# Hybrid decoder step: block-diagonal level scores, step widths in column strips, regrouped banks, vector loads on another queue

## The chip, the cores and the metric

One core of one Trainium2 chip runs the kernel. The metric is device microseconds of one execution. TensorE (PE) multiplies, VectorE (DVE), ScalarE (ACT) and GpSimd (POOL) work on elements, and SyncE (SP) issues DMAs. The engines run side by side and meet only at semaphores.

## The reference

Two decoder layers run over a prompt of 256 tokens and 8 sample sequences of 4 tokens, 288 tokens together. Everything is float32. Each layer has three token mixers on the same normalised input (HGRN2, Mamba-2 SSD, dilated attention), an output projection, and then a dense SwiGLU (layer 0) or top-2-of-8 experts (layer 1). The parts that the change touches:

```python
fgate = lb + (1.0 - lb) * sigmoid(hf)                  # HGRN2: S_t = diag(f_t) S_{t-1} + k_t v_t^T
rel = where(causal, G[:, :, None] - G[:, None, :], -inf)    # G = cumsum(log f)
attn = einsum('bthd,bshd,btshd->bhts', q, k, exp(rel))      # scores within a chunk
...
dt = softplus(dt_raw + dt_bias)                        # SSD step width, dt_raw = 8 columns of h @ w_in
y, s_ssm = ssd_recurrence(xs, dt, -exp(a_log), bm, cm, ssm_h0)
...
qg, kg = rms_norm(q, q_norm[g]), rms_norm(k, k_norm[g])     # attention, groups g = 0, 1, 2
```

## The kernel before

Features lie on partitions and tokens along the free dimension, so a product of one weight tile with all tokens is a matmul with a 128x128 stationary tile and 288 moving columns. A float32 matmul appears in the trace as two instructions, each with its own weight load.

**The mixer loop.** `mixer(L)` on TensorE runs over 70 projection tiles t (`proj_tile`, L960: eight matmuls, 16 instructions) and after each tile does the small products that belong to it (`small_products`, L1257). Two tiles share a weight slab of 1 MB, and four slabs circulate in a ring that SP fills. Constants at the top (L56 to L60) say after which t each small product comes. The other engines run their own loops in the same order, so the schedule is written by hand. Results go into eight PSUM banks: tiles rotate through banks 5 to 7 (`acc_job`), small products have fixed banks 0 to 4 (`plan_mixer`, L322). `open_bank` (L922) waits until the bank's previous content has been read (`drained`), and `close_bank` tells readers that it is filled.

**Level scores (t = 19 to 33).** The HGRN2 scores are exact without large exponents because they are built by levels of distance h = 1, 2, 4, ..., 128 (`LEVELS`). For level i DVE computes distances and multiplies the queries (`hgrn_levels`, L2291), ACT takes the exponential (`level_decay`, L1818), POOL multiplies the keys (L862), and TensorE multiplies keys with queries in `level` (L1021): two blocks of 128 tokens, four heads, each 128x128. DVE then copies the wanted entries from PSUM under a mask (`level_mask`, L2274, `copy_predicated`). The mask of level h has ones only inside diagonal blocks of 2h tokens, and the "same" product (distance 0, t = 20) only on the diagonal. Levels 0, 1 and "same" have a further part for the sample tokens. Level 7 (h = 128) is a product of one block with the other.

**Step widths (t = 27).** `contract(("dt", L), wdt, ...)` (L1481) multiplies the eight columns of the step widths with all 288 tokens in eight matmuls. ACT copies the result (L2038), and DVE starts on it in `dt_start` (L2380).

**Second means and token rows (t = 47 to 51).** `hgrn_means` at 47, then `qk_means` (L1249) of attention group 1 at 48. ACT makes its squares at t = 47 (`qk_squares`, L1907), right behind `hgrn_rstd`, and its inverse roots at t = 48 (`qk_rstd`). At 50 `ssd_x_rows` turns x into token rows, three blocks in banks 3, 4, 3. At 51 `ssd_b_rows` (L1151) turns B, three blocks in banks 0, 1, 2, and makes two products "cb" in banks 3 and 4. DVE reads all of these in `ssd_rows` (L2398), after `qk_normed(L, 1)`.

**Start.** SP issues three loads of x, then 28 small loads of vectors (L636 to L651), then the first four weight slabs (L608), `wdt` and the convolution state. TensorE turns x and then the vectors, ACT copies both out of PSUM, DVE multiplies x with the gain (L2219), and `proj_tile` 0 needs these gained tiles and the first slab. POOL builds constants meanwhile (L796 to L844).

Of the kernel before, what the change touches and what calls it, by code (L numbers as in the profile page):

```python
# [56 lines left out]
AT_HEAD, AT_QK, AT_HG_MEAN = (38, 40, 43, 45), (42, 48, 62), 47  # L57
AT_XTOK, AT_BTOK, AT_EVENT, AT_SSM_ST, AT_STATE, AT_SSM_MEAN, AT_KV = 50, 51, 52, 54, (55, 58, 61, 64), 67, 69
QK_BANKS = ((4, 0, 2, 1), (4, 0, 2, 1), (0, 1, 2, 3))
# [24 lines left out]
def hybrid_decoder(nc, x_prompt, x_sample, state_hgrn, state_ssm, state_conv, cache_kv_w128, cache_kv_w512,  # L84
# [6 lines left out]
    with ctx:  # L91
# [141 lines left out]
        halfm = sb("halfm", [P, DB // 2])  # L233
        own_row = sb("own_row", [P, 2, 4 * DS])
# [87 lines left out]
        def plan_mixer(L):  # L322
            job(("norm", L, 0), 0)
            for t in range(N_PROJ):
# [5 lines left out]
                if t == AT_DT:  # L330
                    acc_job(("dt", L))
                i = (t - AT_LEVEL) // 2
# [34 lines left out]
                if t == AT_XTOK:  # L367
                    for b in range(3):
                        job(("xtok", L, b), 3 + b % 2)
                if t == AT_BTOK:  # L370
                    for b in range(3):
                        job(("btok", L, b), b)
# [225 lines left out]
        def _(sp):  # L598
# [37 lines left out]
            for L in range(DEPTH):  # L636
                vr = arena[:, 3 * D + P * L:3 * D + P * L + P]
                rows = [(V_MIX, mix_norm[L].rearrange("(a p) -> a p", p=P)),
                        (V_FFN, ffn_norm[L].rearrange("(a p) -> a p", p=P)),
                        (V_CW, ssm_conv_w[L].rearrange("j (a p) -> (j a) p", p=P)),  # L640
                        (V_CB, ssm_conv_b[L].rearrange("(a p) -> a p", p=P)),
                        (V_SN, ssm_norm[L].rearrange("(a p) -> a p", p=P)),
                        (V_HN, hgrn_norm[L:L + 1, :]),
                        (V_LB, hgrn_lb_logits[L].rearrange("(a p) -> a p", p=P))]
                for r, src in rows:
                    sp.dma_start(vr[r:r + src.shape[0], :], src).then_inc(vecs_in, 16)  # L646
                for r, src in ((V_QN, att_q_norm[L]), (V_KN, att_k_norm[L])):
                    for e in range(2):
                        sp.dma_start(vr[r:r + AG, 64 * e:64 * e + 64], src).then_inc(vecs_in, 16)
                for k, src in enumerate((ssm_dt_bias, ssm_a_log, ssm_d)):  # L650
                    sp.dma_start(hv[:, L, k:k + 1], src[L].rearrange("(h a) -> h a", a=1)).then_inc(vecs_in, 16)  # L651

            for L in range(DEPTH):
# [129 lines left out]
        def _(pool):  # L783
# [22 lines left out]
            for i, h in enumerate(LEVELS[:7]):  # L806
# [14 lines left out]
                                  pattern=[[DS, DB]], channel_multiplier=-1))  # L821
# [2102 lines left out]
```

## Time and profile before

| | us |
|---|---|
| median of 3 runs (2321.06 to 2325.76) | 2322.9 |
| the profiled execution, as timed | 2326.01 |
| its span in the trace | 2324.3 |
| TensorE busy in the span | 2278.7 (98%) |
| mean granted TensorE clock | 0.992 of full speed |

The profiled execution's time is its span and 1.7 us around it. The rows further down are lines of this one execution. A timeline row gives start, duration, engine, line of the kernel, operation, what it writes and reads with shapes (partitions x elements), how many instructions it merges, and in brackets how long the engine had been idle before it and who ended that. L935 and L941 are the helpers through which all matmuls go, L1794 that of all activations, so what a row is has to be read from its shapes and its place.

### The profile page before, as it was taken

To read this page: it belongs to the slowest core of one execution; us is meant where nothing else is said; L and a number is where in the kernel's file an instruction comes from. 1 tells how busy PE (TensorE), PEld (TensorE's weight loads), DVE (VectorE), ACT (ScalarE), POOL (GpSimd) and SP (SyncE) were. 2 spreads that over 40 slices of the span, in tenths; PEclk is the share of its full clock that TensorE was granted. 3 is DMA by queue.
4 is the path that set the end of the run, shared out by engine and by line. 5 is a ranking of instruction groups with operands and counts; after the bars stand their busy time and mean duration, and the time that the engine had idled before them with its cause. 6 is when DMAs were issued, how large, how long until landed. Compare 5 with 4: busy or idle time off the path is not lost.

```text
span 2324.3 us, 43998 instructions
## 1 busy us (share of the span) xinstructions
PE 2278.7 (98%) x19656; PEld 1454.2 (63%) x19656; DVE 580.8 (25%) x1141; ACT 410.8 (18%) x777; POOL 132.3 (6%) x149
## 2 busy tenths in 40 slices
PE   8999999999999999999999989999999999999998
PEld 6777777767777778777776744354444534353535
DVE  4384324432110127633253210101010010101000
ACT  3323324301000132332331110000000000000000
POOL 2121120000000002111100000000000000000000
PEclk9999999989999999999999999999999999999999
DMA  4334536564444543343476099999999899989993
GB/s 153 125 105 132 151 121 171 140 181 127 131 135 112 153 138 109 118 145 105 136 202 188 19 383 412 418 381 341 384 375 377 339 364 396 361 344 360 396 364 119
DMA packets 290396, 535.20 MB, mean 230 GB/s; under 512 B 10936, under 2 KB 222010, under 8 KB 273824
## 3 DMA queue, kind: packets, MB, share of 16 engines
q1 hardware_dynamic: 290208, 532.38, 64.9%
q8 instruction: 156, 2.56, 0.4%
q14 instruction: 32, 0.26, 0.0%
HBM read 518.50 MB, written 13.85 MB: 229 GB/s over the span
## 4 chain that ended last, share of the span: by engine, by line
PE 94%; DVE 3%; ACT 1%; issue 1%; DMA 1%; SPq 1%; DVEq 0%; ACTq 0%
PE bank L935 91%; PE bank L941 3%; ACT mem L1794 1%; DMA mem<-in_cache_kv_w_dram 0%; DVE mem L2500 0%; DVE col L2503 0%; DVE mem L2471 0%; DVE mem L2204 0%; DVE mem L2513 0%; DMA mem<-in_w_in_dram 0%; DVE mem L2516 0%; ACT L1794 0%; SPq L628 0%; SPq L646 0%; DVE mem L2208 0%
## 5 line engine op out<-in xcount | busy, mean ns | idle before, releaser
L935 PE MATMUL bank<-mem 128*32 128x256 f32 (+9 forms) x11424 | 1054.4, 416 | 19.7 <-DVE mem L2831 5.2
L935 PEld LDWEIGHTS bank<-mem 128*32 128x32 f32 (+3 forms) x11424 | 623.1, 124 | 418.1 <-issue 223.3
L935 PE MATMUL bank<-hflat,mem 128*128 128x288 f32 (+1 forms) x2896 | 713.3, 407 | 0.0
L935 PEld LDWEIGHTS bank<-hflat,mem 128*128 128x128 f32 (+1 forms) x2896 | 536.0, 189 | 160.4 <-issue 18.0
L1794 ACT ACTIVATE mem<-bank 128x288 f32<-128x288 f32 (+7 forms) x441 | 195.5, 462 | 1298.9 <-PE bank L935 745.1
L935 PE MATMUL bank<-mem,steps 128*32 128x384 f32 (+1 forms) x3072 | 292.7, 540 | 0.0
L935 PEld LDWEIGHTS bank<-mem,steps 128*32 128x32 f32 x3072 | 98.2, 110 | 183.2 <-issue 182.3
L2204 DVE TENSOR_TENSOR xT<-xT,bank 128x288 f32<-128x288 f32 x72 | 28.4, 450 | 481.9 <-PE bank L935 481.9
L2208 DVE SCALAR_TENSOR_TENSOR mem<-mem,bank 128x288 f32<-128x288 f32 (+1 forms) x93 | 43.2, 479 | 242.3 <-ACT mem L1794 204.2
L941 PE MATMUL bank<-ident,mem 128*128 128x128 f32 (+3 forms) x642 | 89.3, 273 | 9.8 <-DMA mem<-in_x_sample_dram 6.9
L941 PEld LDWEIGHTS bank<-ident,mem 128*128 128x128 f32 (+3 forms) x642 | 68.9, 143 | 37.2 <-issue 24.9
L1794 ACT ACTIVATE mem<-mem 128x1152 f32<-128x1152 f32 (+8 forms) x103 | 80.5, 781 | 57.1 <-DVE mem L2272 33.0
L2204 DVE TENSOR_TENSOR mem<-mem 128x1152 f32<-128x1152 f32 (+5 forms) x65 | 71.4, 1099 | 10.4 <-POOL mem L862 5.2
L2211 DVE SCALAR_TENSOR_TENSOR mem<-mem,bank 128x384 f32<-128x384 f32 (+1 forms) x45 | 21.4, 505 | 168.6 <-PE bank L935 168.6
L862 POOL TENSOR_TENSOR mem<-mem 128x1152 f32<-128x1152 f32 (+1 forms) x16 | 43.5, 2717 | 263.0 <-ACT mem L1794 147.8
L1794 ACT ACTIVATE hflat<-bank 128x512 f32<-128x512 f32 (+1 forms) x40 | 19.6, 554 | 217.6 <-PE bank L935 217.6
L1794 ACT ACT_TABLE_LOAD x41 | 52.6, 1283 | 6.0 <-PE bank L935 4.0
L2211 DVE SCALAR_TENSOR_TENSOR hflat<-hflat,bank 128x512 f32<-128x512 f32 x24 | 15.1, 683 | 125.5 <-PE bank L935 125.5
L2208 DVE SCALAR_TENSOR_TENSOR hflat<-hflat,bank 128x512 f32<-128x512 f32 x24 | 15.1, 683 | 109.8 <-ACT hflat L1794 109.8
L1794 ACT ACTIVATE hflat<-xT 128x288 f32<-128x288 f32 x24 | 10.6, 443 | 148.1 <-DVE xT L2204 86.3
L935 PEld LDWEIGHTS bank<-mem,hflat 32*128 32x128 f32 (+2 forms) x432 | 24.9, 182 | 17.8 <-issue 11.9
L935 PE MATMUL bank<-mem,hflat 32*128 32x288 f32 (+2 forms) x432 | 34.3, 397 | 1.5 <-ACT hflat L1794 1.0
(213 smaller groups left out, 779.0 us busy)
## 6 DMA issues: line engine op xcount, KB each, us to landing
mem<-in_w_moe_up_dram SPq DMA_DIRECT2D x64, 2048.0 KB, 10.0
mem<-in_w_moe_down_dram SPq DMA_DIRECT2D x56, 2048.0 KB, 10.3
mem<-in_w_moe_up_dram SPq DMA_DIRECT2D x32, 2304.0 KB, 10.5
mem<-in_w_in_dram SPq DMA_DIRECT2D x70, 1024.0 KB, 5.1
mem<-in_w_moe_up_dram SPq DMA_DIRECT2D x16, 1536.0 KB, 8.7
mem<-in_w_ffn_up_dram SPq DMA_DIRECT2D x44, 512.0 KB, 5.1
mem<-in_cache_kv_w_dram SPq DMA_DIRECT2D x26, 512.0 KB, 5.7
mem<-in_w_ffn_down_dram SPq DMA_DIRECT2D x16, 704.0 KB, 5.0
```

The costliest lines, as they stand in the source:

```text
L862: say(gp.tensor_tensor(kt[:, :, 0:w], hgp[:, 4:8, 0:w], dist[:, :, 0:w], ALU.mult), "lvl_k", L, i + 1)
L935: return mm(out, lhsT, rhs, start=start, stop=stop, skip_group_check=True)
L941: return nc.tensor.transpose(out, in_, ident[0:k, 0:k])
L1794: return nc.scalar.activation(out, in_, f, **kw)
L2204: return ve.tensor_tensor(out, a, b, op)
L2208: return ve.scalar_tensor_tensor(out, tanh, 1.0, b, ALU.add, ALU.mult)
L2211: return ve.scalar_tensor_tensor(out, a, 0.5, b, ALU.mult, op)
```

## The change

- `level` multiplies only diagonal blocks: 32 wide for h up to 16 and for "same", 64 wide for h = 32, and for h = 64 the one block 64x64 that its mask wants. In layer 0, level 0 and "same" stay 128 wide.
- The eight matmuls of the step widths go to four strips of output partitions, two each (`step_widths`). ACT copies all 128 partitions, and at t = 29 one matmul with a new constant `fourth` adds the strips, which ACT copies again. `fourth` costs POOL one memset and four selects at the start.
- Means of group 1 move from t = 48 to 49, into banks 0, 1, 2, 4. Token rows of x use banks 3, 4, 0, those of B banks 1, 2, 0, with the third block of B behind the "cb" products. DVE does `qk_normed(L, 1)` between reading the rows of x and the "cb" products.
- The 28 vector loads go from SP's queue to ACT's, ahead of everything else that ACT does.

```diff
-AT_HEAD, AT_QK, AT_HG_MEAN = (38, 40, 43, 45), (42, 48, 62), 47
+AT_HEAD, AT_QK, AT_HG_MEAN = (38, 40, 43, 45), (42, 49, 62), 47
-QK_BANKS = ((4, 0, 2, 1), (4, 0, 2, 1), (0, 1, 2, 3))
+QK_BANKS = ((4, 0, 2, 1), (0, 1, 2, 4), (0, 1, 2, 3))
@@ plan_mixer
+                if t == AT_DT + 2:
+                    acc_job(("dt_sum", L))
@@
-                        job(("xtok", L, b), 3 + b % 2)
+                        job(("xtok", L, b), (3, 4, 0)[b])
-                        job(("btok", L, b), b)
+                        job(("btok", L, b), (1, 2, 0)[b])
@@ sync
-            for L in range(DEPTH):
-                vr = arena[:, 3 * D + P * L:3 * D + P * L + P]
-                rows = [...]
-                for r, src in rows:
-                    sp.dma_start(vr[r:r + src.shape[0], :], src).then_inc(vecs_in, 16)
...
@@ gpsimd
+            step(gp.memset(fourth[:, :], 0.0))
+            for q in range(4):
+                step(gp.affine_select(out=fourth[:, :], in_=fourth[:, :], compare_op=ALU.not_equal, fill=1.0,
+                                      base=-32 * q, pattern=[[-1, SH]], channel_multiplier=1))
@@ tensor, level
+                near = 0 if i == "same" else LEVELS[i]
+                w = P if L == 0 and i in (0, "same") else 32 if near <= 16 else 64
                 for b in range(2):
                     acc = open_bank(("lvl", L, i, b))
                     for h in range(HH):
-                        ins = put(acc[:, P * h:P * h + P], kk[:, h, P * b:P * b + P], qq[:, h, P * b:P * b + P])
+                        for t0 in range(0, P, w):
+                            tk, tq = (t0, t0) if near < 64 else (0, 64)
+                            if near == 64 and t0 > 0:
+                                continue
+                            ins = put(acc[tk:tk + w, P * h + tq:P * h + tq + w], kk[:, h, P * b + tk:P * b + tk + w],
+                                      qq[:, h, P * b + tq:P * b + tq + w])
@@ tensor, ssd_b_rows
-                for b in range(3):
+                for b in range(2):
                     yield from token_rows(("btok", L, b), xs, b, (4, 5))
...
+                yield from token_rows(("btok", L, 2), xs, 2, (4, 5))
@@ tensor
+            def step_widths(L):
+                acc = open_bank(("dt", L))
+                for k in range(KT):
+                    r = 32 * (k % 4)
+                    ins = put(acc[r:r + SH, 0:T], wdt[:, k, :], hT[:, k, :], k < 4, k >= 4)
+                close_bank(ins, ("dt", L))
@@
-                        close_bank(contract(("dt", L), wdt, 0, KT, hT, SH), ("dt", L))
+                        step_widths(L)
+                    if t == AT_DT + 2:
+                        acc = open_bank(("dt_sum", L))
+                        pe.wait_ge(*drained(("dt", L)))
+                        close_bank(put(acc[0:SH, 0:T], fourth[:, :], yall[:, 9, :]), ("dt_sum", L))
@@ scalar
-                        copy_out(yall[0:SH, 9, :], ("dt", L), psum(("dt", L))[0:SH, 0:T])
+                        copy_out(yall[:, 9, :], ("dt", L), psum(("dt", L))[:, 0:T])
+                    if t == AT_DT + 2:
+                        copy_out(yall[0:SH, 9, :], ("dt_sum", L), psum(("dt_sum", L))[0:SH, 0:T])
...
+            for L in range(DEPTH):
+                vr = arena[:, 3 * D + P * L:3 * D + P * L + P]
+                rows = [...]
+                for r, src in rows:
+                    act.dma_start(vr[r:r + src.shape[0], :], src).then_inc(vecs_in, 16)
...
@@ vector
-                dve.wait_ge(*drained(("dt", L)))
+                dve.wait_ge(*drained(("dt_sum", L)))
@@ ssd_rows, between the rows of x and "cb"; taken out ahead of ssd_rows
+                qk_normed(L, 1)
```

## Rows read from the trace of the kernel before

**Rows 1.** The page's first part: busy time, share, instructions of TensorE.
```profile
PE 2278.7 (98%) x19656; PEld 1454.2 (63%) x19656; DVE 580.8 (25%) x1141; ACT 410.8 (18%) x777; POOL 132.3 (6%) x149
```

**Rows 2.** Timeline of TensorE around the second means and token rows, both layers.
```profile
265.78 2.18 PE L935 MATMUL bank<-mem,pairs 128*128 128x288 f32 x8 [1.96 <-ACT mem L1794]
...
277.86 1.08 PE L935 MATMUL bank<-ident,mem 128*32 128x128 f32 x32 [1.27 <-DVE mem L2204]
...
1044.24 2.18 PE L935 MATMUL bank<-mem,pairs 128*128 128x288 f32 x8 [1.96 <-ACT mem L1794]
...
1056.32 1.08 PE L935 MATMUL bank<-ident,mem 128*32 128x128 f32 x32 [1.27 <-DVE mem L2204]
```

**Rows 3.** Windows (A:B, length; busy per engine; then clock, DMA share, GB/s).
```profile
128.10:129.88 1.78, 1.78 (x17) 1.78 (x16) 1.67 (x4) 1.26 (x2) 0.00 (x0) 1.00 0.29 55
149.07:153.04 3.97, 3.97 (x17) 1.35 (x16) 3.77 (x4) 0.00 (x0) 2.35 (x1) 1.00 0.73 243
189.62:190.63 1.01, 1.01 (x33) 0.81 (x32) 0.44 (x1) 0.94 (x2) 0.00 (x0) 1.00 0.00 0
464.41:464.71 0.30, 0.30 (x32) 0.26 (x24) 0.00 (x0) 0.00 (x0) 0.00 (x0) 1.00 0.00 0
490.00:505.00 15.00, 12.63 (x58) 9.30 (x59) 4.39 (x12) 0.00 (x0) 0.00 (x0) 0.55 0.34 124
```

**Rows 4.** TensorE groups by shape, whole span: stationary rows*columns, moving shape, count, busy, mean.
```profile
L935 PE MATMUL bank<-mem 128*64 128x128 f32 x176 | 22.3, 277 | 0.0
...
L935 PE MATMUL bank<-hflat,wdt 128*8 128x288 f32 x32 | 8.1, 406 | 0.0
...
L935 PE MATMUL bank<-mem 128*32 128x32 f32 x104 | 4.4, 198 | 0.0
```

**Rows 5.** Timeline of VectorE from level 2's mask to level 3's, layer 0.
```profile
130.74 1.51 DVE L2289 COPY_PREDICATED mem<-lmask,bank 128x512 f32<-128x512 uint32 x2
...
132.29 3.52 DVE L2204 TENSOR_TENSOR mem<-mem 128x1152 f32<-128x1152 f32 x2
...
139.46 1.50 DVE L2289 COPY_PREDICATED mem<-lmask,bank 128x512 f32<-128x512 uint32 x2
```

**Rows 6.** Timeline of ScalarE and VectorE around the second means, layer 0.
```profile
261.98 1.28 ACT L1794 ACT_TABLE_LOAD   x1
263.28 2.36 ACT L1794 ACTIVATE mem<-mem 128x1152 f32<-128x1152 f32 x2
...
272.56 2.18 DVE L2471 SCALAR_TENSOR_TENSOR mem<-mem,vecs 128x288 f32<-128x288 f32 x4 [5.21 <-ACT mem L1794]
...
276.39 4.32 DVE L2204 TENSOR_TENSOR mem<-bank,mem 128x512 f32<-128x512 f32 x6 [1.65 <-PE bank L941]
```

**Rows 7.** Timeline of the start: issues, copies, gains, first tile, last constant.
```profile
2.20 0.37 SPq L646 DMA_DIRECT2D mem<-in_mix_norm_dram  x1
...
8.00 0.60 ACT L1794 ACTIVATE xT<-bank 128x512 f32<-128x512 f32 x1 [5.91 <-PE bank L941]
...
10.62 1.27 ACT L1794 ACTIVATE xT<-bank 128x512 f32<-128x512 f32 x3 [0.26 <-PE bank L941]
...
11.08 0.30 SPq L651 DMA_DIRECT2D hv<-in_ssm_d_dram  x1
...
11.42 5.12 SPq L608 DMA_DIRECT2D mem<-in_w_in_dram  x4
...
12.83 0.64 ACT L1794 ACTIVATE vecs<-bank 128x16 f32<-128x16 f32 x3 [0.95 <-PE bank L941]
...
13.50 3.21 DVE L2219 TENSOR_SCALAR mem<-xT,vecs 128x288 f32<-128x288 f32 x8 [13.50 <-ACT vecs L1794]
...
16.57 2.92 SPq L662 DMA_DIRECT2D wdt<-in_w_in_dram  x1
16.61 6.88 PE L935 MATMUL bank<-mem 128*128 128x288 f32 x16 [2.71 <-DMA mem<-in_w_in_dram]
...
18.53 0.15 POOL L844 IOTA mem<- 128x32 int32 x1
```

More of the change, by code:

```diff
@@ L233, in hybrid_decoder @@
         halfm = sb("halfm", [P, DB // 2])
+        fourth = sb("fourth", [P, SH])
         own_row = sb("own_row", [P, 2, 4 * DS])
@@ L636, in _ @@
             for L in range(DEPTH):
-                vr = arena[:, 3 * D + P * L:3 * D + P * L + P]
[L638 to L644, printed above, removed]
-                for r, src in rows:
-                    sp.dma_start(vr[r:r + src.shape[0], :], src).then_inc(vecs_in, 16)
[L647 to L651, printed above, removed]
-            for L in range(DEPTH):
                 ag = first_slab[L] + NS_HG + NS_SSM
@@ L2089, in dense @@
                     fn(e, psum(key)[:, 0:T], ACT.Tanh, scale=0.5).then_inc(up_exp, 1)
+            for L in range(DEPTH):
+                vr = arena[:, 3 * D + P * L:3 * D + P * L + P]
+                rows = [(V_MIX, mix_norm[L].rearrange("(a p) -> a p", p=P)),
+                        (V_FFN, ffn_norm[L].rearrange("(a p) -> a p", p=P)),
+                        (V_CW, ssm_conv_w[L].rearrange("j (a p) -> (j a) p", p=P)),
+                        (V_CB, ssm_conv_b[L].rearrange("(a p) -> a p", p=P)),
+                        (V_SN, ssm_norm[L].rearrange("(a p) -> a p", p=P)),
+                        (V_HN, hgrn_norm[L:L + 1, :]),
+                        (V_LB, hgrn_lb_logits[L].rearrange("(a p) -> a p", p=P))]
+                for r, src in rows:
+                    act.dma_start(vr[r:r + src.shape[0], :], src).then_inc(vecs_in, 16)
+                for r, src in ((V_QN, att_q_norm[L]), (V_KN, att_k_norm[L])):
+                    for e in range(2):
+                        act.dma_start(vr[r:r + AG, 64 * e:64 * e + 64], src).then_inc(vecs_in, 16)
+                for k, src in enumerate((ssm_dt_bias, ssm_a_log, ssm_d)):
+                    act.dma_start(hv[:, L, k:k + 1], src[L].rearrange("(h a) -> h a", a=1)).then_inc(vecs_in, 16)
             for b, (t0, n) in enumerate(BLK):
@@ L2591, in mixer @@
                 hgrn_norm_out(L)
-                qk_normed(L, 1)
                 ssd_rows(L)
```

## The prediction

> **What bounds the kernel now.** I read the busy line first: TensorE is busy 98% of the span and no other engine over 25% [rows 1]. So a microsecond counts only if it is TensorE's own work or its idle time. Next I read the timeline of TensorE through one mixer and through the other. Between the level stage (t = 19 to 33) and the token rows it runs without a gap, tile after tile. Around t = 48 to 50 it stands still twice in each layer: 1.96 us before the means of group 1, ended by ScalarE, and 1.27 us before the third block of the token rows of x, ended by VectorE [rows 2]. Last I read the start, where TensorE's first projection tile begins at 16.61 and was released by the weight DMA [rows 7]. These three places are what the change touches. For each edit the question is what it takes off TensorE's path, and whether another engine is then late.
>
> **Level scores, the largest term.** A level now is 2 blocks x 4 heads = 8 matmuls, 16 instructions, and takes 1.78 us (first window of [rows 3]), 111 ns for each instruction of 128 moving columns. The change makes four blocks of 32 of each: 32 matmuls, 64 instructions, each with 32 stationary and 32 moving columns. Whether that is cheaper hangs on whether blocks on different output partitions run side by side. The row that answers is the stretch at 464.41, where the last sample scores do just this, 24 instructions of 128*32 by 32 columns going round the four strips: 0.30 us with the gap to the next work (fourth window of [rows 3]), or 12.5 ns each. At that price a level costs 64 x 12.5 = 0.80 us. That scales the gap at the end too, which comes once. From below: the turns at 189.62 go round the four strips with 128 moving columns in 1.01 us for 32 instructions (third window of [rows 3]), 31.6 ns each, a quarter of that for 32 columns is 7.9 ns, and 64 of them are 0.51 us. I take 0.65 us, between the two since one gap belongs to it. Saved: 1.13 us. It applies to levels 1 to 4 of layer 0 and to "same" and levels 0 to 4 of layer 1, ten products: 11.3 us (bounds 9.8 and 12.7). Sample parts stay.
>
> Level 5 gets two blocks of 64, level 6 one. The nearest row is the group 128*64 by 128 columns, 176 instructions in 22.3 us [rows 4], 127 ns each with one strip in use, so 63 ns for 64 columns. Level 6 has 16 instructions on one strip, 1.0 us. Level 5 has 32 on two strips, side by side again 1.0 us. Each saves 0.78, four of them 3.1 us. Together the levels give **14.4 us**.
>
> At this place a rule speaks against the change. The Trainium skill, TensorEngine Tiling (Array Packing), Instruction Overhead, gives each matmul about 60 cycles of overhead and says not to take a tiling factor from a dimension that is already small. 64 instructions at 60 cycles of 2.4 GHz one behind another would be 1.6 us, and a level would save only 0.2. The trace differs: 24 such instructions took 0.30 us [rows 3], half of what 60 cycles each would make, so this overhead overlaps between strips.
>
> **Does another engine become late in the level stage?** TensorE's period per level falls from 9.54 us (two tiles of 3.97 us, and 1.78) to about 8.6. VectorE's own period is 8.72 us, from one level's mask to the next with no idle marked inside [rows 5]. So VectorE is the slower one by 0.1 us per level, while levels 2 to 4 last. But TensorE does not need VectorE's mask for the next level, it needs the multiplied queries, and these are the first thing after the mask: about 1.4 us of the pair at 132.29 [rows 5], ready by 133.7, while TensorE wants them at 137.6 (128.10 and one period). That is about 4 us of slack, against which a backlog of some tenths per level is set. At levels 5 and 6 VectorE had idle time, since the step widths gave it 3.97 us (second window of [rows 3]). These shrink, and level 6 has nine extra small copies on VectorE (`new_conv_rows`, L2357). Following the order of its work through, I find the queries of level 7 two to three microseconds early. I cost this at nothing, and the rival below prices it.
>
> **Step widths.** Eight matmuls of eight columns take 3.97 us (second window of [rows 3]), the same 8.1 us for both layers by the group [rows 4]. In four strips, 16 instructions become four rounds of 243 to 250 ns (3.97 over 16), about 1.0 us, with 0.1 for the end. The adding matmul at t = 29 costs two more instructions, 0.5 us. Saved 2.4 us per layer, **4.8 us**. Its wait for ScalarE's copy is put two tiles (8 us) behind the product, and the copy is of 0.4 us, so it is met. Behind that waiting instruction stands the next tile. VectorE reads the widths only after level 7, so the later arrival is hidden by the level stage. ScalarE's second copy of 0.4 us has idle time around it.
>
> **Second means and token rows.** ScalarE's chain behind `hgrn_means` is four logarithms, a table load at 261.98, an exponential and the squares in one row of 2.36 us that ends at 265.64 [rows 6], and TensorE starts at 265.78. One tile later TensorE would come to these means at about 267.8 on a time line without the stall (265.78 - 1.96 = 263.8, and one tile). ScalarE now puts the gate tile of t = 48 (0.41 us) between exponential and squares, so the squares end at about 266.1. That is 1.7 us early: the **1.96 us** go. What is late next is the token rows of x at t = 50, at 273.8. Their banks 3, 4 and 0 must be drained, 4 and 0 by the logarithms of group 1. These follow a gate tile at 267.9 and a table load of 1.28, and take 0.5 us each, so they end at about 271.7, 2 us early. The third block no longer waits for VectorE's reading of the first, so the **1.27 us** go too. The "cb" products at about 280.4 need banks 3 and 4 drained. VectorE reads three blocks in 4.32 us [rows 6] from 274.4 on, the first two by 277.3, so they are met. Then `qk_normed` takes 2.18 us [rows 6] and is over before the "cb" products are filled. The third block of B reaches ScalarE some 1.7 us later in relation to the tiles, and behind it waits POOL, whose first product for TensorE is several microseconds away. Two layers, **6.5 us**.
>
> **Start.** SP spends 2.20 to 11.38 on the vectors, a pitch of (11.08 - 2.20)/27 = 0.33 us, and only then issues the slabs, of which the first releases TensorE at 16.61 [rows 7]. With the vectors gone the slab is there before 9 us. The path turns to ScalarE: a table load to about 2.1 (of 1.28 us, as the one in [rows 6]), 28 issues, six copies of x, three of vectors. No DMA of ScalarE's queue is in the trace. SP's pitch is the nearest row: 28 x 0.33 = 9.2, to 11.3. The copies of x, three of 0.60 and three in 1.27, take 3.2 with gaps, to 14.5, the vectors 0.64, to 15.1, the first gain 0.4 [rows 7]. TensorE starts at 15.6, **1.0 us** earlier. Bounds: with issues that cost next to nothing ScalarE copies x as now and TensorE starts at about 13.1, 3.5 us earlier. If the small loads crowd with the slabs' 4 MB, whose issues take 1.28 each and the one behind them 2.92 [rows 7], the start is later than now; I price a doubled pitch, 8 us. POOL's five extra instructions delay the last constant from 18.7 to about 20.5. It is wanted after the first tile, at 22.4.
>
> The Trainium skill, DMA: Bandwidth & Descriptors, Issuing engines are not separate DMA queues, says that issuing from several engines saves only sequencer time. Here that time is the whole 9.2 us that SP spends [rows 7], so rule and plan agree, and what is left is who pays it.
>
> **The sum.** 14.4 + 4.8 + 6.5 + 1.0 = 26.7 us. The profiled execution took 2326.0, so 2299.3. It is 3.1 above the median of the runs, and I keep that difference: **2296**. From the mixers on, everything is tied to TensorE and moves as a block, with no gain or loss.
>
> **Rivals.**
> - *VectorE sets the pace of the levels.* For: its period of 8.72 against 8.6, and the extra copies at level 6. Against: the 4 us of slack. Price: five periods per layer held at 8.9 instead of 8.6 and one wait of 1 us at level 7, 2.5 us per layer, 2301.
> - *Strips do not run side by side.* For: the group of 128*32 by 32 columns has a mean of 42 ns over 104 instructions, 80 of them one behind another in one strip [rows 4]. At 31 ns each a level of 64 costs 2.0 us, 0.3 more than now (ten: 3). Level 5 loses 0.2 twice, level 6 still gains 1.5. The widths lose 0.5 per layer. The sum is 6.5 + 1.0 - 3 + 1.1 - 1 = 4.6 us, so 2318. The skill's overhead rule, as above, would lead near here: levels at 1.6 us. Against: the third and the fourth window of [rows 3].
> - *The start is late.* Doubled pitch on ScalarE, 28 x 0.66, start at 24.8, 8 us later than now instead of 1 earlier: 2305.
> - *The whole is slower.* If each of ScalarE's 28 issues costs what SP's issue behind the slabs costs, 2.92 [rows 7], ScalarE is held to 84, TensorE starts at 88 instead of 16.6, and the run takes 2296 + 1 + 72 = 2369. The price from which this decides is 1.3 us per issue, start at 42.7. Against: SP's own small loads at 0.33 behind 1.1 MB of x.
> - *The start is better.* Issues cheap: 2294.
>
> **How the numbers follow.** Forecast 0.62, better start 0.10, VectorE 0.10, late start 0.11, strips serial 0.04 (of which half counts as no change), whole slower 0.02, and 0.01 else. The bounds of the levels (1.5 either way) and of the clock widen it. The clock fell to its lower level of 1.2 GHz in the stretch 490 to 505 (mean granted 0.55) after TensorE had waited [rows 3], and where such stretches fall against the work moves a run by a few microseconds, as the spread of 4.7 us among the three runs allows. The range 2289 to 2306 holds forecast, better start, VectorE and the most of the late start. A measurement of this kernel can tell about 0.2% from no change, 4.6 us. Faster 0.95, within 0.02, slower 0.03.
>
> **What would show it.** Level rows of 64 instructions in 0.5 to 0.8 us on TensorE, and 16 of them at level 6 in 1.0. Step widths in about 1.1 us. No idle time marked before the means of group 1 and before the token rows. TensorE's first tile at 15.6, released by VectorE instead of the DMA. Idle time on TensorE released by VectorE or POOL at a level would make the prediction wrong, as would DMA issues on ScalarE of over 0.5 us, or levels of over 1.2 us.

## The result and the profile after

The changed kernel takes 2306.9 us (median of 4 runs, 2306.6 to 2309.3), against 2324.3 us of the kernel before beside it (4 runs, 2321.1 to 2325.9). The ratio is 0.9928, 95% interval 0.9915 to 0.9941. That is faster, but 17.4 us faster and not the 26.7 of the sum, and 0.9 us outside the range. The profiled execution took 2306.64 us, its span is 2304.9, 19.4 us less than before.

The busy line of the changed kernel, the answer to [rows 1]:

```profile
PE 2257.9 (98%) x20172; PEld 1433.9 (62%) x20172; DVE 587.9 (26%) x1141; ACT 411.4 (18%) x779; POOL 133.7 (6%) x154
```

TensorE's work fell by 20.8 us. VectorE's rose by 7.1 us with the same 1141 instructions, though the change gives it no more to do. The timeline of TensorE through levels 2 to 7 of layer 0, then the lines with idle time of the same stage in layer 1 (start, duration, instructions merged, idle time before and who ended it):

```profile
126.47 0.76 PE L925 MATMUL bank<-mem 128*32 128x32 f32 x64
127.16 8.03 PE L925 MATMUL bank<-hflat,mem 128*128 128x288 f32 x32
135.38 0.76 PE L925 MATMUL bank<-mem 128*32 128x32 f32 x64 [0.20 <-DVE mem L2232]
...
145.55 0.76 PE L925 MATMUL bank<-mem 128*32 128x32 f32 x64 [1.45 <-DVE mem L2232]
146.16 1.16 PE L925 MATMUL bank<-hflat,wdt 128*8 128x288 f32 x16
147.25 8.03 PE L925 MATMUL bank<-hflat,mem 128*128 128x288 f32 x32
155.21 1.15 PE L925 MATMUL bank<-mem 128*64 128x64 f32 x32
156.29 0.65 PE L925 MATMUL bank<-mem,fourth 128*8 128x288 f32 x2
156.87 8.03 PE L925 MATMUL bank<-hflat,mem 128*128 128x288 f32 x32
164.82 1.15 PE L925 MATMUL bank<-mem 128*64 128x64 f32 x16
...
175.94 1.16 PE L925 MATMUL bank<-mem 128*128 128x128 f32 x8 [2.02 <-DVE mem L2232]
...
900.63 0.76 PE L925 MATMUL bank<-mem 128*32 128x32 f32 x64 [0.83 <-DVE mem L2232]
...
910.79 0.76 PE L925 MATMUL bank<-mem 128*32 128x32 f32 x64 [1.45 <-DVE mem L2232]
...
941.27 1.19 PE L925 MATMUL bank<-mem 128*128 128x128 f32 x8 [2.09 <-DVE mem L2232]
```

Read the starts: a level of 64 instructions takes 0.69 us (126.47 to 127.16) where it took 1.78 [rows 3], a level of 64-wide blocks 1.08. The step widths take 1.09 and 0.58 for the sum. All about as costed. Yet six waits for VectorE's multiplied queries have come up where the kernel before had none: 0.20, 1.45, 2.02, 0.83, 1.45 and 2.09, together 8.0 us. And behind the last one the clock fell, as this window shows (columns as in [rows 3]; the clock is the third number from the end):

```profile
942.20:952.00 9.80, 9.80 (x38) 7.43 (x37) 9.29 (x15) 2.63 (x8) 2.62 (x1) 0.83 0.15 52
```

Two tiles, 32 instructions, took 9.62 us there instead of the 7.93 behind level 7 of layer 0, 1.7 us more.

The two stalls of [rows 2] are gone in both layers. The means of group 1 and the token rows of x, with nothing in brackets:

```profile
263.59 2.10 PE L925 MATMUL bank<-mem,pairs 128*128 128x288 f32 x8
...
270.38 1.08 PE L925 MATMUL bank<-ident,mem 128*32 128x128 f32 x32
...
1030.60 2.10 PE L925 MATMUL bank<-mem,pairs 128*128 128x288 f32 x8
...
1037.39 1.08 PE L925 MATMUL bank<-ident,mem 128*32 128x128 f32 x32
```

The start, the answer to [rows 7]: first and last of ScalarE's 28 issues, its table load, its copies of x, VectorE's gain, TensorE's first and third product.

```profile
0.80 0.60 ACTq L2113 DMA_DIRECT2D mem<-in_mix_norm_dram  x1
...
10.96 0.32 ACTq L2118 DMA_DIRECT2D hv<-in_ssm_d_dram  x1
11.31 1.28 ACT L1804 ACT_TABLE_LOAD   x1 [11.31 <-issue]
12.60 3.10 ACT L1804 ACTIVATE xT<-bank 128x512 f32<-128x512 f32 x6
...
16.61 3.48 DVE L2247 TENSOR_SCALAR mem<-xT,vecs 128x288 f32<-128x288 f32 x8 [16.61 <-ACT vecs L1804]
17.13 5.87 PE L925 MATMUL bank<-mem 128*128 128x288 f32 x16
...
26.71 4.04 PE L925 MATMUL bank<-mem 128*128 128x288 f32 x16
```

The issues cost (10.96 - 0.80)/27 = 0.38 us each, somewhat over the 0.33 of SP, and the table load comes behind them. The first tile begins at 17.13, 0.5 later than before. It then runs faster (5.87 instead of 6.88 us), and the tile at 26.71 stood at 27.21 before: 0.5 us gained on balance. The granted clock over this tile is 0.50 up to 20.62, and its first 8 of 16 instructions start 0.48 us apart, and then it is full and they start 0.24 apart. In the kernel before 11 instructions are 0.48 apart. Its trace has no change of the clock on record there.

**Where VectorE's time went.** One level of VectorE, ScalarE and POOL in the changed kernel, level 2's distance to level 3's:

```profile
126.60 1.36 DVE L2300 SCALAR_TENSOR_TENSOR mem<-mem 128x1152 f32<-128x1152 f32 x1
...
128.47 3.94 DVE L2378 SCALAR_TENSOR_TENSOR mem<-mem,vecs 128x312 f32<-128x312 f32 x3
...
129.35 2.73 POOL L852 TENSOR_TENSOR mem<-mem 128x1152 f32<-128x1152 f32 x1 [6.79 <-ACT mem L1804]
...
132.45 1.49 DVE L2317 COPY_PREDICATED mem<-lmask,bank 128x512 f32<-128x512 uint32 x2
133.97 2.75 DVE L2232 TENSOR_TENSOR mem<-mem 128x1152 f32<-128x1152 f32 x2
...
136.75 1.36 DVE L2300 SCALAR_TENSOR_TENSOR mem<-mem 128x1152 f32<-128x1152 f32 x1
```

The same place in the kernel before:

```profile
129.01 1.70 DVE L2350 SCALAR_TENSOR_TENSOR mem<-mem,vecs 128x312 f32<-128x312 f32 x3
...
130.22 2.99 POOL L862 TENSOR_TENSOR mem<-mem 128x1152 f32<-128x1152 f32 x1 [7.12 <-PE bank L935]
```

The period is 10.15 us (126.60 to 136.75), where it was 8.72 [rows 5]. The three convolution operations take 3.94 us and not 1.70. Look at who released POOL. Before, it waited for TensorE: POOL overwrites the keys only when the level's product has read them (`level_end`). With the short product it is released by ScalarE's exponential, 0.88 us behind the start of the convolution row (128.47 to 129.35) where it was 1.21 (129.01 to 130.22). The third convolution operation, with two inputs in SBUF, begins about 1.15 behind that start. Before, this was just ahead of POOL. Now it is 0.28 behind POOL, and the operation is held until POOL is through: it ends at 132.41, POOL at 132.08. The bracket of POOL's row names who released it, and VectorE's long operation counts as busy, so no idle time shows the hold. The two engines meet here without a semaphore between them. Over the whole span, VectorE's group of these operations in the changed kernel, and the one of before (last columns: busy, mean ns | idle before):

```profile
L2378 DVE SCALAR_TENSOR_TENSOR mem<-mem,vecs 128x312 f32<-128x312 f32 x48 | 47.0, 980 | 1.7
```

```profile
L2350 DVE SCALAR_TENSOR_TENSOR mem<-mem,vecs 128x312 f32<-128x312 f32 x48 | 26.2, 545 | 1.7
```

20.8 us more in this group, and only 7.1 in all. The rest is given back, because the hold is not new. In the kernel before, POOL's multiplication held VectorE at every one of these levels, only elsewhere. It held the first multiplication of the queries in the pair of [rows 5] (2.13 us for 1.36, so 3.52 for the pair, where the changed kernel's takes 2.75) and at the levels after it (the first takes 2.62 and twice 2.74 us). At level 6 it held one of the nine small copies, 2.23 us for 0.18:

```profile
171.45 3.72 DVE L2361 COPY mem<-mem 128x24 f32<-128x24 f32 x8
...
172.58 2.35 POOL L862 TENSOR_TENSOR mem<-mem 128x1024 f32<-128x1024 f32 x1 [7.18 <-PE bank L935]
```

In the changed kernel all of these have their short times again: 4.1 us less in the multiplications of 128x1152, 6.1 in those of 128x1024 and 4.1 in the copies. What is new is that POOL now catches an operation that comes earlier, and so holds VectorE for 2.0 to 2.2 us per level where it was 0.8 to 2.1.

### The profile page after: what moved, and what is told of

Read it like the earlier page. It is cut to its first block, busy times and chain, and to the rows that moved or that the text cites. A ratio compares the mean times of both kernels' runs of the same rounds, so it can differ in the third digit from the quotient of the medians.

```text
span 2304.9 us, 45045 instructions
## 1 busy us (share of the span) xinstructions
PE 2257.9 (98%) x20172; PEld 1433.9 (62%) x20172; DVE 587.9 (26%) x1141; ACT 411.4 (18%) x779; POOL 133.7 (6%) x154
## 3 DMA queue, kind: packets, MB, share of 16 engines
q8 instruction: 160, 2.62, 0.5%
## 4 chain that ended last, share of the span: by engine, by line
PE 90%; DVE 8%; ACT 1%; issue 1%; ACTq 0%; DMA 0%; DVEq 0%
PE bank L925 86%; PE bank L931 4%; DVE mem L2232 2%; DVE mem L2378 2%; DVE mem L2317 1%; DVE mem L2300 1%; ACT mem L1804 0%; DVE mem L2236 0%; DVE mem L2529 0%; DVE col L2532 0%; DVE mem L2500 0%; DVE mem L2542 0%; DVE mem L2545 0%; ACTq L2113 0%; DVE mem L2375 0%
## 5 line engine op out<-in xcount | busy, mean ns | idle before, releaser
L925 PE MATMUL bank<-mem 128*32 128x256 f32 (+10 forms) x11936 | 1036.3, 405 | 23.6 <-DVE mem L2232 10.6
L925 PEld LDWEIGHTS bank<-mem 128*32 128x32 f32 (+3 forms) x11936 | 605.2, 122 | 424.7 <-issue 225.1
L1804 ACT ACTIVATE mem<-bank 128x288 f32<-128x288 f32 (+8 forms) x443 | 196.3, 461 | 1237.8 <-PE bank L925 683.7
L2232 DVE TENSOR_TENSOR mem<-mem 128x1152 f32<-128x1152 f32 (+5 forms) x65 | 61.3, 943 | 10.1 <-POOL mem L852 5.2
L2378 DVE SCALAR_TENSOR_TENSOR mem<-mem,vecs 128x312 f32<-128x312 f32 x48 | 47.0, 980 | 1.7
```

Source lines behind the costliest of these rows:

```text
L925: return mm(out, lhsT, rhs, start=start, stop=stop, skip_group_check=True)
L1804: return nc.scalar.activation(out, in_, f, **kw)
L2232: return ve.tensor_tensor(out, a, b, op)
L2378: ins = ve.scalar_tensor_tensor(cv[:, m, 0:CW], xpad[:, m, j:j + CW], w[j], cv[:, m, 0:CW], ALU.mult, ALU.add)
```

## The experiments

The theory was that POOL's key multiplication now begins ahead of a VectorE operation with two SBUF inputs and holds it. The first rival was that VectorE simply has too much work for a period of 8.6 us, whatever POOL does. Each ratio below is to the kernel before on the same chip, with its 95% interval. The changed kernel stands at 0.9928 (0.9915 to 0.9941). The experiments ran on three chips, where the kernel before had medians of 2325.8 to 2327.0, against 2324.3 beside the changed kernel. By that spread a difference of two medians is good to about 3 us, and by the intervals one of two ratios to about 5. Both are estimates, and what the traces show decides where it can.

**Levels in full width again.** The rest of the change stays.

```diff
-                w = P if L == 0 and i in (0, "same") else 32 if near <= 16 else 64
+                w = P
+                near = min(near, 32)
```

> The changed kernel with the level scores 128 wide again, all else as changed. Collision theory (POOL's key multiply, released earlier since TensorE is faster, holds up VectorE's last convolution step, and VectorE then holds up TensorE): TensorE's period per level is 9.5 us again, POOL is released by TensorE again, the third convolution step takes 0.55 us instead of 2.8, and the idle times of TensorE ahead of levels 3, 4 and 7 (8.0 us in both layers, and 1.7 us of low clock behind one of them) are gone. The levels cost 13.7 us more, so about 4 us slower than the changed kernel: 2311. Work theory (VectorE simply has too much to do for the shorter period): the same time, 2311, since VectorE's own period of 8.7 fits into 9.5; the third step then would not change its duration.

Measured 2311.4 us, ratio 0.9952 (0.9933 to 0.9970). The convolution and POOL in this kernel:

```profile
128.59 1.70 DVE L2379 SCALAR_TENSOR_TENSOR mem<-mem,vecs 128x312 f32<-128x312 f32 x3
...
129.81 2.98 POOL L852 TENSOR_TENSOR mem<-mem 128x1152 f32<-128x1152 f32 x1 [7.12 <-PE bank L925]
```

POOL is released by TensorE again, the operations are back at 1.70 us, and TensorE waits at no level. So the short products move the collision onto the convolution. Of their 13.7 us the change kept 4.5 by the medians (2311.4 to 2306.9) and 13.7 - 9.7 = 4.0 by the terms. In the traces the two level stages together are 2.7 us shorter in the changed kernel than here. The time alone does not part the theories, which both gave 2311. The length of the third operation does.

**Keys multiplied on VectorE.** POOL's loop over the levels goes, and VectorE gets 1.36 us more per level.

```diff
+                    say(tt(kt[:, :, 0:w], hgp[:, 4:8, 0:w], dist[:, :, 0:w], ALU.mult), "lvl_k", L, i + 1)
```

> The changed kernel, with the multiply of the keys of each level moved from POOL to VectorE, right behind the multiply of the queries. VectorE gets 1.36 us of work more per level. Collision theory: nothing of POOL runs beside the convolution, the third step takes 0.55 us, VectorE's period is 1.5 + 4 x 1.36 + 2.2 = 9.1 us instead of 10.1, TensorE's idle time in the level stages falls from 8.0 us to 1 to 3, and the kernel takes 2299 to 2302. Work theory: the period rises from 10.1 to 11.4, TensorE waits 6 us more in each layer, 2318 or above.

Measured 2301.1 us, ratio 0.9906 (0.9888 to 0.9923). This is the run that parts the two theories: VectorE has more to do and is less late. Its convolution takes 1.70 us, its period 9.37 (127.63 to 137.00), and the waits marked on TensorE at the levels are 0.35, 0.68, 0.23, 0.67 and 0.68, 2.6 us and not 8.0. By the amount of work alone it would have become slower.

```profile
129.50 1.70 DVE L2372 SCALAR_TENSOR_TENSOR mem<-mem,vecs 128x312 f32<-128x312 f32 x3
...
145.00 0.76 PE L918 MATMUL bank<-mem 128*32 128x32 f32 x64 [0.68 <-issue]
```

The profile names no releaser for the 2.6 us that stay. They fit a period of 9.37 that is still too long for TensorE: its levels stand 9.39 apart (135.61 to 145.00), and 8.65 where TensorE does not wait (mask order, below).

**POOL's multiplication at half its length.** It leaves out half of the keys' products in all levels but the first of layer 0.

```diff
+                    u = w if L == 0 and i == 0 else w // 2
-                    say(gp.tensor_tensor(kt[:, :, 0:w], hgp[:, 4:8, 0:w], dist[:, :, 0:w], ALU.mult),
+                    say(gp.tensor_tensor(kt[:, :, 0:u], hgp[:, 4:8, 0:u], dist[:, :, 0:u], ALU.mult),
```

> The changed kernel, with POOL multiplying the keys of only half of the tokens of each level (level 0 of layer 0 in full), so the scores of the other half come from keys of an earlier level. VectorE's instructions are all unchanged. Collision theory: POOL's multiply takes 1.3 us instead of 2.7, VectorE's blocked step ends 1.3 us sooner, its period is 8.8 us and TensorE's idle time in the level stages falls to under 2 us: 2298 to 2301. Work theory: VectorE has the same to do, and TensorE waits the same 8 us: 2307.

```profile
126.89 2.73 DVE L2379 SCALAR_TENSOR_TENSOR mem<-mem,vecs 128x312 f32<-128x312 f32 x3
...
127.77 1.51 POOL L853 TENSOR_TENSOR mem<-mem 128x576 f32<-128x576 f32 x1 [6.78 <-ACT mem L1805]
```

Measured 2295.9 us, ratio 0.9877 (0.9858 to 0.9896). POOL is shorter by 1.22 us (1.51 for 2.73), and the convolution row by 1.21 (2.73 for 3.94). So VectorE's third operation follows POOL's end, one for one. TensorE waits at no level.

**Mask copies ahead of the last convolution operation.** For levels 2 to 6 VectorE does the mask, which reads PSUM, before the third operation. No work is added or left out.

```diff
                 for j in range(1, CONV):
+                    if j == CONV - 1 and before_last is not None:
+                        before_last()
...
-                    if i >= 2:
+                    if 2 <= i < 7:
+                        convolve(L, i - 2, lambda: level_mask(L, i))
+                    elif i == 7:
                         convolve(L, i - 2)
...
-                    level_mask(L, i)
+                    if i < 2 or i == 7:
+                        level_mask(L, i)
```

> The changed kernel, with VectorE copying a level's masked scores ahead of the last of the four convolution steps instead of behind it (levels 2 to 6), so that 1.5 us of reading PSUM lie where POOL's multiply runs. The same instructions on every engine. Collision theory: the copies from PSUM are not held up, the last step is held for 0.9 us instead of 2.2, VectorE's period is 8.8 us instead of 10.1, TensorE's idle time in the level stages falls to under 2 us: 2298 to 2301. Work theory: the order of the same work changes nothing, 2307.

```profile
129.28 1.12 DVE L2383 SCALAR_TENSOR_TENSOR mem<-mem,vecs 128x312 f32<-128x312 f32 x2
...
130.16 2.75 POOL L852 TENSOR_TENSOR mem<-mem 128x1152 f32<-128x1152 f32 x1 [6.78 <-ACT mem L1804]
130.44 1.51 DVE L2317 COPY_PREDICATED mem<-lmask,bank 128x512 f32<-128x512 uint32 x2
131.99 1.26 DVE L2383 SCALAR_TENSOR_TENSOR mem<-mem,vecs 128x312 f32<-128x312 f32 x1
```

Measured 2297.8 us, ratio 0.9894 (0.9875 to 0.9912). The copies run beside POOL at their usual length, and of the third operation only 0.7 us of waiting are left (1.26 for 0.55). The period is 8.66 and the waits at the levels are gone. A change of order alone gives 9.1 us by the medians and 7.9 by the ratios. In the traces the two level stages are 10.5 us shorter than in the changed kernel, where 8.0 of waits and 1.7 of low clock stood. With the hold out of TensorE's way the interval of the ratio holds what the prediction gave for the change (2296 / 2322.9 = 0.9884).

**The sign on ScalarE.** VectorE's -|d| (1.36 us) goes, ScalarE does an `Abs` (1.16 us) and an exponential of the negative.

```diff
-                say(fn(dist[:, :, 0:w], dist[:, :, 0:w], ACT.Exp), "lvl_decay", L, i + 1)
+                step(fn(dist[:, :, 0:w], dist[:, :, 0:w], ACT.Abs))
+                say(fn(dist[:, :, 0:w], dist[:, :, 0:w], ACT.Exp, scale=-1.0), "lvl_decay", L, i + 1)
...
-                say(ve.scalar_tensor_tensor(d, d, -1.0, d, ALU.mult, ALU.min), "lvl_dist", L, i + 1)
```

> The changed kernel with the sign of the level distances on ScalarE: VectorE's operation of 1.36 us on 128x1152 goes, and ScalarE takes the absolute value (1.16 us as its exponential) ahead of the exponential of the negated value. The collision theory: POOL's multiply now starts 2.4 us behind VectorE's distances instead of 1.3 us behind its last operation, and VectorE's convolution (0.44 and three of 0.55) is over by 2.1 us, so the third operation is back at 0.55, POOL runs beside the mask copies, the waits of TensorE at the levels are gone and the time is 2299 us or below. If VectorE's collision only moved to its next two-input operation, waits of 0.2 to 1.5 us stay and the time is 2303 to 2307.

```profile
127.54 1.70 DVE L2378 SCALAR_TENSOR_TENSOR mem<-mem,vecs 128x312 f32<-128x312 f32 x3
...
129.61 2.65 POOL L852 TENSOR_TENSOR mem<-mem 128x1152 f32<-128x1152 f32 x1 [6.59 <-ACT mem L1804]
130.82 4.04 DVE L2233 TENSOR_TENSOR mem<-mem 128x1152 f32<-128x1152 f32 x2
```

Measured 2297.7 us, ratio 0.9867 (0.9850 to 0.9883). Both readings of the expectation came partly true. The convolution is back at 1.70 us, and the collision did move: the pair of multiplications takes 4.04 and not 2.75 us, the first of them held until POOL's end at 132.26. VectorE has 1.36 us less to do, so that it costs TensorE nothing, and no wait at a level is left.

**Step widths as before.** Eight matmuls in one strip again, 2.3 us more work on TensorE per layer.

```diff
-                        step_widths(L)
+                        close_bank(contract(("dt", L), wdt, 0, KT, hT, SH), ("dt", L))
```

> The changed kernel with the step widths as before: eight matmuls of eight columns one behind another at t = 27, 3.97 us instead of 1.09 and 0.58. By the sizes alone TensorE gets 2.3 us more work per layer and the time is 2306.9 + 4.6 = 2311.5 us. My theory says that VectorE was late there, so that TensorE waited 2.0 us at level 7 of each layer in the changed kernel: with 2.3 us more work ahead of it this wait falls to nearly nothing, the wait of 1.45 us at the level ahead of the step widths stays, and the time is about 2306.9 + 0.6 = 2307.5.

```profile
146.09 0.76 PE L923 MATMUL bank<-mem 128*32 128x32 f32 x64 [1.45 <-DVE mem L2224]
146.70 4.04 PE L923 MATMUL bank<-hflat,wdt 128*8 128x288 f32 x16
...
176.60 1.05 PE L923 MATMUL bank<-mem 128*128 128x128 f32 x8
```

Measured 2305.2 us, ratio 0.9911 (0.9895 to 0.9928). The wait at level 7 is gone in both layers, the waits at levels 3 and 4 stay. Followed through both traces, the level stage of layer 0 is as long as in the changed kernel to 0.1 us, and that of layer 1 is 1.7 us shorter, since no low clock follows it. The strips of the step widths work as costed and bring nothing in this kernel: what TensorE saves at t = 27 it waits out at t = 33.

**Old banks and order of the second means.** The constants, banks and calls of the third part of the change are put back.

```diff
-AT_HEAD, AT_QK, AT_HG_MEAN = (38, 40, 43, 45), (42, 49, 62), 47
+AT_HEAD, AT_QK, AT_HG_MEAN = (38, 40, 43, 45), (42, 48, 62), 47
-QK_BANKS = ((4, 0, 2, 1), (0, 1, 2, 4), (0, 1, 2, 3))
+QK_BANKS = ((4, 0, 2, 1), (4, 0, 2, 1), (0, 1, 2, 3))
```

> The changed kernel with the second means back at t = 48, the token rows of x in banks 3, 4, 3 and those of B in 0, 1, 2 ahead of the 'cb' products. My theory: this part was worth the two stalls it removed, 1.96 and 1.27 us in each layer, and nothing of it was given back, so both stalls come back at their old sizes and the time is 2306.9 + 6.5 = 2313.4 us. The rival, that the stalls were only moved and are waited out elsewhere (the experts, the projection), gives 2307 with the stalls back.

```profile
262.50 2.18 PE L925 MATMUL bank<-mem,pairs 128*128 128x288 f32 x8 [1.95 <-ACT mem L1803]
...
274.58 1.08 PE L925 MATMUL bank<-ident,mem 128*32 128x128 f32 x32 [1.27 <-DVE mem L2231]
```

Measured 2315.4 us, ratio 0.9957 (0.9941 to 0.9973). That is 8.5 us above the changed kernel by the medians and 0.0029, 6.7 us, by the ratios, where 6.5 were expected. Both stalls are back, to 0.01 us, in both layers. This part of the gain is whole, and somewhat more than the stalls: from the tiles ahead of the means to those behind the "cb" products each layer takes 3.86 us more than in the changed kernel, where the stalls make 3.22. Between the kernel before and the changed one it is 3.86 too.

**Levels alone.** Step widths, banks, order and vector loads as before, only the blocks of `level` changed (the edit is the part of the change's diff at `tensor, level`; the constant `fourth` is still built on POOL, but nothing uses it).

> The kernel before with the block-wise levels alone: step widths, banks, order of the means and vector loads as before. By the sizes on TensorE alone it is 13.7 us below the kernel before, 2310.6 us. My theory: VectorE, held up beside POOL's multiply, keeps its period of 9.5 to 10.1 us here too. Waits of 0.2, 1.45, and in layer 1 0.8 and 1.45 us, come back as in the changed kernel, 3.9 us together, and the wait at level 7 stays away because the old step widths give VectorE 2.3 us more. That makes 2324.3 - 13.7 + 3.9 = 2314.5 us.

Measured 2313.8 us, ratio 0.9949 (0.9934 to 0.9964). TensorE waits 0.20 and 1.45 us in layer 0 and 0.83 and 1.45 in layer 1, the same numbers as in the changed kernel, and not at level 7. The third operation is held for 2.0 to 2.2 us at three levels of each layer and then no more: the long step widths at t = 27 give VectorE time to catch up. The collision with the convolution belongs to the short levels, not to their meeting with another part.

**Vector loads split.** Layer 0's 14 loads on SP, layer 1's 14 on ScalarE.

```diff
@@ sync
+            for L in (0,):
+                ...
@@ scalar
-            for L in range(DEPTH):
+            for L in (1,):
```

> The changed kernel with the 14 small loads of layer 0 on SP's queue as before and only the 14 of layer 1 on ScalarE's. My theory: the time of the start is the sum of issues on one queue ahead of the copies of x (28 at 0.38 us on ScalarE). With 14 there, ScalarE is free at 0.8 + 14 x 0.38 = 6.1 and after its table load at 7.4, copies x by 10.7, and TensorE's first tile begins at about 13.1 instead of 17.1; SP issues its slabs 4.6 us later than in the changed kernel and still ahead of that. At the lower clock a tile at the start takes up to 1.7 us longer, so 3 us of the 4 are left: 2304 us. The rival, that the loads and not their issues are late, leaves the first tile at 17 and the time at 2307.

```profile
5.77 1.28 ACT L1820 ACT_TABLE_LOAD   x1 [5.77 <-issue]
...
13.29 6.73 PE L941 MATMUL bank<-mem 128*128 128x288 f32 x16
```

Measured 2304.4 us, ratio 0.9904 (0.9888 to 0.9921). The first tile begins at 13.29 (13.1 expected) and takes 6.73 us and not 5.87. The third product begins at 24.04 and not 26.71, so 2.7 of the 3.8 us are left, and 2.5 show in the medians (5.6 by the ratios). Ten of the tile's instructions are 0.48 us apart here and 8 in the changed kernel. The start of the first tile followed the number of issues ahead of ScalarE's copies, as the sum had it.

**Both together, and with the sign on ScalarE as well.** The mask order and the split loads, then the same with the `Abs` edit.

> The changed kernel with the level's mask copies ahead of the last convolution operation and with the vector loads split, layer 0's 14 on SP and layer 1's 14 on ScalarE. Each alone measured 2297.8 and 2304.35 against 2306.9 of the changed kernel. They touch different places, so the gains add: 2306.9 - 9.1 - 2.5 = 2295.3 us. If the earlier start is spent at the lower clock, 2298.

Measured 2292.95 us (2292.24 to 2293.15), ratio 0.9853 (0.9836 to 0.9869).

> The same two edits and the sign of the level distances on ScalarE besides, 1.36 us less for VectorE and 1.16 more for ScalarE per level. My theory: with the mask copies moved nothing waits for VectorE at the levels any more, so less work for it is worth nothing: 2295.3 us as without it. If waits for VectorE are left that are hidden in the timeline's small gaps, up to 2 us less.

Measured 2292.92 us, ratio 0.9853 (0.9836 to 0.9871). The two agree within their spread: once the order of VectorE is right, 1.36 us less of its work per level is worth nothing that these runs show. Mask order and split loads are 14 us below the changed kernel by the medians and 17 by the ratios, where 11.6 were expected, and the sign on ScalarE adds an edit and no speed.

## Why the prediction was wrong

| term | predicted | in the trace |
|---|---|---|
| levels on TensorE | 14.4 | 10 x 1.09 + 4 x 0.70 = 13.7 |
| step widths | 4.8 | 2 x 2.3 = 4.6 |
| second means, token rows | 6.5 | 6.5, stalls gone |
| start | 1.0 | 0.5 |
| VectorE in the level stage | 0 | -8.0 of waits, -1.7 of clock |
| sum | 26.7 | 15.6 |

**The step that failed** is the prediction's answer to whether another engine becomes late in the level stage, "I cost this at nothing". It took VectorE's period as 8.72 us, with a loss of 0.1 us per level against a slack of 4 us at the queries. The period became 10.15 us, so each level lost about 1.5 us against TensorE and not 0.1. POOL was not followed: what would its multiplication wait for once the product ahead of it is 1.09 us shorter? Its row said that TensorE released it, and the next candidate, ScalarE's exponential, ends only 0.5 us before that (129.75 against 130.22 in the kernel before).

The slack was misread as well. "About 1.4 us of the pair" put the queries of level 3 at 133.7. But the pair of [rows 5] takes 3.52 us, where two operations of 1.36 would take 2.75: the first was held already and ended at 134.42. And "TensorE wants them at 137.6" is one old period behind the old start of level 2. In the changed kernel TensorE is ready for level 3 at 135.18, 2.5 us earlier, since the levels ahead of it are short too. The queries end at 135.33, and the first wait, 0.20, is there at once.

The rival "VectorE sets the pace" had the right engine and the price too small. It held the periods at 8.9, 2.5 us per layer, 5 in all, against 9.7 measured, and its reason was VectorE's amount of work, which the run with the keys on VectorE speaks against. Its 2301 is still 6 us from the result. Its wait at level 7 was right in kind (2.02 and 2.09, priced 1). The last paragraph of the prediction named idle time of TensorE released by VectorE at a level as what would make it wrong, and that is what came.

The Trainium skill, SBUF — State Buffer, Who interferes with whom, states that a VectorE instruction with two SBUF inputs contends with a GpSimd instruction that reads SBUF, and calls the port pair that the two engines share "an exclusive lock". That who issues first has the pair for the whole instruction while the other "fully blocks" it says of VectorE's two-port modes. The traces show the same for the two-input operations here. The held operation of 128x312 ended 0.33, 0.34 and 0.34 us behind POOL (changed kernel, half multiplication, mask order), whether POOL took 2.73, 1.51 or 2.75. The prediction did not weigh this section, the one that bore on its zero.

**The levels.** 0.69 us was inside the bounds (0.51 to 0.80) and near the 0.65 taken. The row of 24 instructions round four strips was the right one to read. The trace has 10.8 ns for each of 64 instructions, and the rival of serial strips falls. That rival was priced at 31 ns an instruction, for which it names no row; the 42 ns of its own row would have made its price 2.7 us a level. The 60 cycles for each matmul of the Trainium skill, TensorEngine Tiling (Array Packing), Instruction Overhead, would be 1.6 us for a level, so the measurement speaks against them where strips alternate.

But what a level saves is not what its own row saves. TensorE's period fell from 9.54 us to 8.65 (mask order, 127.28 to 135.93), 0.89 and not 1.09, because the two tiles behind a short level take longer up to the next level, 7.96 us (147.25 to 155.21) where they took 7.76 (129.88, the end of the first window of [rows 3], to 137.64):

```profile
137.64 1.95 PE L935 MATMUL bank<-mem 128*128 128x128 f32 x16
```

The prediction had the difference before it: it took the period from 9.54 to about 8.6 and the level's saving as 1.13.

**Step widths.** The size was right to 0.1 us per layer, the worth was not. They shortened the one stretch in which VectorE caught up, and the run with the old step widths is no slower. What they are worth with the mask order no run shows.

**Second means and token rows.** Right in both stalls, both ways: gone in the changed kernel, back when undone. The stretch as a whole gained 3.86 us per layer, 7.7 and not 6.5. The 0.6 us per layer beyond the stalls come from the new order and were in no term.

**Start.** The chain through ScalarE was the right one, and the size of an issue was off: 0.38 us and not 0.33, 28 x 0.05 = 1.4 of the 1.5 us by which 17.13 is later than 15.6. That the table load came behind the issues and not ahead of them changes the order and not the sum. Against that the first tile was 1.0 us shorter, with 8 and not 11 of its instructions at the slower pace, which the term had left out.

**What the sum leaves open.** By the rows of the table the span should fall by 15.6 us, and it fell by 19.4. Following the same work through both traces gives the stages whole: 0.5 us at the start, 7.0 in the two level stages, 7.7 in the two stretches of second means and token rows, and 4.1 between 460 and 530. So the level stages gained even less than the table's 13.7 + 4.6 - 9.7 = 8.6, and the 4.1 us between 460 and 530 stand in no term. The kernel before waits 1.58 us for a load of the cache at 491 and the changed one doesn't, and between 480 and 510 the granted clock is 0.89 of full speed where it was 0.77. In the traces of the experiments this wait is 0.3 to 2.9 us in five and absent in the others, with most of the change in nearly all of them, so the change alone does not settle it, and the cause stays open. Without these 4.1 us the result would lie further outside the range, so that it came within 1 us of it is in part luck. The medians differ by 17.4.

## What to carry over

When a product is shortened, ask not only which engine is next late, but whose release it was: an engine that starts earlier may now run beside another that it holds up. In the profile, two operations of one kind and shape with different durations are the mark of such a collision, worth following before any slack is counted on. And a saving ahead of an engine that is late is no saving: here 4.6 us less work on the step widths bought nothing as long as VectorE was late, and moving one operation behind two copies bought 8 to 10.

## What the runs showed of the hardware

- VectorE's operation with two SBUF inputs beside POOL's multiplication isn't slowed in proportion. It waits for POOL's end and does most of its work behind it: 128x312 ended 0.33 to 0.34 us behind it in three kernels (0.55 alone), 128x1152 about 1.2 us behind it in two, the kernel before and the one with the sign on ScalarE (1.36 alone).
- A plain copy of 128x24 from SBUF to SBUF, one input, was held too: 2.23 us for 0.18, ending 0.03 behind POOL's 174.93 in the kernel before. `copy_predicated` from PSUM beside POOL took its usual 0.75 us.
- POOL was held too. Where POOL's multiplication of 128x1152 began while a VectorE operation had 0.49 us left, it took 2.99 us, where 0.25 were left 2.73, and with only a `copy_predicated` beside its start 2.64.
- Which of the two came first decided, and a shift of a third of a microsecond was enough: the third operation of the convolution kept its 0.55 us where it began 0.06 ahead of POOL (kernel before), and took 2.8 us where it began 0.28 behind (changed kernel).
- 64 matmul instructions of 32x32 blocks round four strips of output partitions took 0.69 us, 10.8 ns each, and those of 64 columns on two strips (32) or one (16) both 1.08 us.
- The first tile at the start took 6.88, 5.87 and 6.73 us when begun at 16.61, 17.13 and 13.29 us. Behind a wait of 2.09 us at 941 two tiles took 9.62 us and not 7.93, and behind a wait of 2.02 us at 176 they did not.
